# Stick-breaking attention dealt out between the rounds of a chunked recurrence, with the residual X kept in device memory meanwhile

## The reference

```python
h = h + 0.5 * swiglu(rms_norm(h, ffn1_norm), ...)             # feed-forward 1
proj = rms_norm(h, mix_norm) @ w_in
sb_out = stick_breaking_attention(q, k, v)                    # 8 heads of 64
rw_out = rwkv7_time_mix(proj[..., 3 * SB_WIDTH:], ...)        # 8 heads of 64
h = h + concatenate([sb_out, rw_out], -1) @ w_out
h = h + 0.5 * swiglu(rms_norm(h, ffn2_norm), ...)             # feed-forward 2

# stick-breaking attention, per block of queries
z = q_blk @ k.T * scale
log_keep = where(valid, -softplus(z), 0.0)
log_rest = cumsum(log_keep, reverse=True) - log_keep
attn = where(valid, exp(log_sigmoid(z) + log_rest), 0.0)
out = attn @ v

# rwkv7: a state S (64 x 64) per head, one step per token
sa = S @ -kk_t
S = S * w_t + outer(sa, kk_t * a_t) + outer(v_t, k_t)
y_t = S @ r_t
```

## Time and profile before

| what | us |
|---|---|
| median of 3 runs | 2483.41 (2479.57 to 2485.19) |
| profiled execution | 2484.07 |
| its span | 2482.1 |
| attention (559.27 to 614.27) | 55.00 |
| recurrence (614.27 to 738.67) | 124.40 |

### The profile page before, as it was taken

One profiled execution on the slowest core, in us unless ns is written; L12 is line 12 of the kernel. 1 busy time (PEld: TensorE's weight loads), 2 busy tenths in 40 slices (PEclk: granted clock), 3 DMA queues, 4 the chain that ended last, 5 costly groups with the idle time before them and its releaser, 6 DMA issues.

```text
span 2482.1 us, 48923 instructions
## 1 busy us (share of the span) xinstructions
PE 2433.5 (98%) x20393; PEld 2237.6 (90%) x20393; DVE 1706.8 (69%) x2927; ACT 1080.4 (44%) x1956; POOL 98.8 (4%) x108
## 2 busy tenths in 40 slices
PE   9999999999999999999999999999989999999998
PEld 7999999996887989898999999898877888989896
DVE  6877775646556879688879585243976445879694
ACT  5444343334434535356535243112874224535252
POOL 0000001000320000001000002000000000000001
PEclk9999999999999999999999999999999999999999
DMA  4233232220001332332232323222212323233322
GB/s 151 85 106 104 99 99 92 78 84 6 4 12 43 104 109 96 111 96 78 81 122 94 101 96 97 78 86 84 60 43 77 98 94 102 94 102 103 102 92 71
DMA packets 72378, 213.00 MB, mean 86 GB/s; under 512 B 12796, under 2 KB 20028, under 8 KB 72032
## 3 DMA queue, kind: packets, MB, share of 16 engines
q1 hardware_dynamic: 70496, 209.03, 26.0%
q0 software_dynamic: 480, 0.73, 0.1%
q10 hardware_dynamic: 1184, 0.12, 0.0%
HBM read 207.61 MB, written 2.20 MB: 85 GB/s over the span
## 4 chain that ended last, share of the span: by engine, by line
PE 87%; DVE 6%; ACT 4%; issue 2%; DMA 0%; DVEq 0%; ACTq 0%
PE PS L866 22%; PE PS L1401 20%; PE PS L1358 11%; PE PS L1360 11%; PE PS L1359 11%; DVE WL L951 1%; ACT WH L939 1%; PE PS L1236 1%; PE PS L2259 1%; PE PS L1709 1%; PE PS L1708 1%; PE PS L1710 1%; PE PS L2842 1%; DVE P L2905 1%; PE PS L2209 1%
## 5 line engine op out<-in xcount | busy, mean ns | idle before, releaser
L1358 PE MATMUL PS<-OPH,WH 128*128 128x256 f32 (+1 forms) x2112 | 604.5, 286 | 3.8 <-DVE OPL L1108 2.8
L1360 PE MATMUL PS<-OPH,WL 128*128 128x256 f32 (+1 forms) x2112 | 600.6, 284 | 0.0
L1359 PE MATMUL PS<-OPL,WH 128*128 128x256 f32 (+1 forms) x2112 | 598.9, 284 | 0.0
L939 ACT ACTIVATE WH<-WR 128x1024 fp32r<-128x1024 f32 (+2 forms) x277 | 275.5, 995 | 564.0 <-PE PS L866 272.6
L951 DVE TENSOR_TENSOR WL<-WR,WH 128x1024 fp32r<-128x1024 f32 (+2 forms) x277 | 318.7, 1151 | 190.1 <-ACT WH L939 190.0
L1358 PEld LDWEIGHTS PS<-OPH,WH 128*128 128x128 f32 x2112 | 402.1, 190 | 7.6 <-DVE OPL L1108 3.0
L1359 PEld LDWEIGHTS PS<-OPL,WH 128*128 128x128 f32 x2112 | 402.0, 190 | 1.9 <-issue 1.5
L1360 PEld LDWEIGHTS PS<-OPH,WL 128*128 128x128 f32 x2112 | 401.4, 190 | 0.0
L939 ACT ACTIVATE WH<-SUMS 128x512 fp32r<-128x512 f32 x352 | 210.9, 623 | 230.7 <-DVE SUMS L977 188.0
L951 DVE TENSOR_TENSOR WL<-SUMS,WH 128x512 fp32r<-128x512 f32 x352 | 234.7, 687 | 21.0 <-ACT WH L939 20.5
L866 PE MATMUL PS<-NHI,WH 128*128 128x264 f32 (+2 forms) x976 | 237.9, 309 | 1.5 <-ACT TMP L2633 1.0
(11 more groups left out here) (476 smaller groups left out, 4627.8 us busy)
## 6 DMA issues: line engine op xcount, KB each, us to landing
WR<-in_ffn_up SPq DMA_DIRECT2D x64, 512.0 KB, 4.0
WR<-in_ffn_down SPq DMA_DIRECT2D x64, 512.0 KB, 3.7
WR<-in_ffn_gate SPq DMA_DIRECT2D x56, 512.0 KB, 3.7
WR_MORE<-in_ffn_gate SPq DMA_DIRECT2D x32, 512.0 KB, 4.5
WR_MORE<-in_ffn_up SPq DMA_DIRECT2D x24, 512.0 KB, 4.1
WR<-in_ffn_down SPq DMA_DIRECT2D x32, 384.0 KB, 3.2
WR<-in_w_gate SPq DMA_DIRECT2D x24, 512.0 KB, 3.5
WR<-in_w_out SPq DMA_DIRECT2D x16, 512.0 KB, 3.6
```

Source lines behind the costliest of these rows:

```text
L939: e.activation(split_unit(i)[0][:, 0:w], src, ACT.Copy).then_inc(S["w_hi"], 1)
L1358: e.matmul(o, wh[:, at:at + 128], hi, start=k == 0 and s in (1, 2, 5), stop=False, skip_group_check=True)
L1359: e.matmul(o, wh[:, at:at + 128], lo, start=False, stop=False, skip_group_check=True)
L1360: last = e.matmul(o, wl[:, at:at + 128], hi, start=False, stop=k == 3, skip_group_check=True)
```

## The change

Attention is no longer a stage. Its sections are lists per round, and the three engines take them from there:

```diff
+        SB_SCANS = [(944, 1344), (0, 416), (416, 944)]
+        SB_DIFFS = [(416, 1343), (0, 416)]
+        BANKS_OF = {"z": 2, "t": 1, "v": 1}
+        ROUNDS, SB_ROUNDS = 4 * 8 + 16, 34
+        for p in range(4):
+            d = 1 + 7 * p
+            for half in range(2):
+                for y in range(4):
+                    breaking_at[d + 3 + 4 * half + y // 2].append(("t", p, half, y))
+            for part in range(2):
+                breaking_at[d + 9 + part].append(("v", p, part, 0))
+            for pos in range(3):
+                breaking_at[max(d - 2 + pos, 0)].append(("z", p, pos, 0))
+            for half in range(2):
+                for piece, late in (("scan", 0), 0), (("scan", 1), 0 + half), (("scan", 2), 1 + half), (("diff", 0), 2 + half), (("diff", 1), 2 + half):
+                    pieces_at[d + 3 * half + late].append((2 * p + half,) + piece)
```

A pair of heads takes seven rounds. The scan is cut in three pieces, the subtraction in two, the value product in two. On ScalarE and VectorE the sections and pieces of a round stand at the start of the next one; the copy into Y_S moves to ScalarE:

```diff
         def act_rwkv(e, q):
             for c, k in mixed_order:
+                if (c, k) in first_of_round:
+                    for item in breaking_at[4 * c + k - 1]:
+                        act_breaking(e, q, *item)
+                if c == 8 and k in (12, 13):
+                    q.wait_ge("outs", 7)
+                    q.wait_ge("sb_val", 4)
+                    act_split(e, q, U["w_out", k - 11])
...
         def dve_rwkv(e, q):
             for c, k in mixed_order:
+                if (c, k) in first_of_round:
+                    for item in pieces_at[4 * c + k - 1]:
+                        dve_breaking(e, q, *item)
+                if (c, k) == (8, 12):
+                    q.wait_ge("outs", 7)
+                    dve_split(e, q, U["w_out", 1])
```

```diff
+            def between_writers(last):
+                fences[0] += 1
+                last.then_inc(S["fence"], 1)
+                if waiting and taken[0] + BANKS_OF[waiting[0][0]] <= 3:
+                    taken[0] += BANKS_OF[waiting[0][0]]
+                    pe_breaking(e, q, *waiting.popleft())
+                q.wait_ge("fence", fences[0])
+
             for c, k in mixed_order:
+                if (c, k) in first_of_round:
+                    while waiting:
+                        pe_breaking(e, q, *waiting.popleft())
+                    waiting.extend(breaking_at[4 * c + k])
+                    taken[0] = 0
...
+                    if x < 4:
+                        for p, f, u in heads_in_turn:
+                            last = e.matmul(PS[f, bank, 64 * p:64 * p + 64], TU[u, 1, p], PM[u, p], start=p == 0,
+                                            stop=True, skip_group_check=True)
+                        between_writers(last)
                     for p, f, u in heads_in_turn:
-                        if x < 4:
-                            e.matmul(PS[f, bank, 64 * p:64 * p + 64], TU[u, 1, p], PM[u, p], start=p == 0,
-                                     stop=True, skip_group_check=True)
-                        last = e.matmul(PS[u, bank + 1, 64 * p:64 * p + 64], PM[u, p], TU[u, 1, p], start=p == 0,
-                                        stop=True, skip_group_check=True)
+                        last = e.matmul(PS[u, bank, 256 + 64 * p:320 + 64 * p], PM[u, p], TU[u, 1, p],
+                                        start=x == 4 and p == 0, stop=True, skip_group_check=True)
```

The first corners of step 1, which were already two runs of eight one after the other, have the same fence between them. The bonus products move to chunk 8:

```diff
+        RK_AT = {(8, 3 + 2 * i): i for i in range(4)}
+        BONUS_AT = {(8, 5 + 2 * i): i for i in range(4)}
```

For the space, X is stored to device memory during the projection and loaded again before the output projection; the values, the scan's result and a turned operand lie in its place. KEEPS (three heads) lies in the four weight slots WR, other tiles in WH and WL, so w_out 1 and 2 are fetched only when the last transposes are made:

```diff
+            for k in range(DT):
+                q.wait_ge("added", k + 1)
+                e.dma_start(x_kept[:, k, :], X[:, k, :]).then_inc(S["x_out"], 16)
+                sync_weights(e, q, shifted + k, shifted + k + 1)
+            sync_weights(e, q, shifted + DT, late)
+            q.wait_ge("x_out", 16 * DT)
+            q.wait_ge("sb_turn", 32)
+            sync_weights(e, q, late, late + 2)
+            q.wait_ge("sb_val", 4)
+            q.wait_ge("sb_diff", 16)
+            q.wait_ge("outs", 4)
+            for k in range(DT):
+                e.dma_start(X[:, k, :], x_kept[:, k, :]).then_inc(S["x_in"], 16)
```

More of the change, by code:

```diff
@@ L11 @@
+import collections
 import itertools
@@ new lines, in build @@
+        SMALL_0, at = place("SMALL0", at, 3, 4, CH)
+        chunk_homes.append(home + [SMALL_0[:, i] for i in range(3)])
+        home, _, at = of_home(1, at)
+        LT1, end = place("LT1", AFTER_TURNED, 4, CH)
+        assert end <= AT_WH + 2 * SLOT
+        VH1, end = place("VH1", AFTER_QK, 4, CH)
+        assert end <= AT_RKV - 4 * L
+        AT_HOME_2 = at
+        PM1, at = place("PM1", AT_HOME_2 + 2304, 4, CH)
+        STT, at = place("STT", at, 4, HD)
+        assert at <= FREE - 192
@@ L573, in build @@
+        RS, SA = (heads_of_rows(flat_tmp[:, 1536 + 256 * i:1792 + 256 * i]) for i in range(2))
+        ST, at = place("ST", AT_WA, 2, 4, HD)
+        assert at <= AT_WA + L
         Y_R, _ = place("Y_R", AT_RKV - 4 * L, 4, L)
-        assert at <= AT_RKV - 4 * L
         CEN, at = place("CEN", AFTER_BONUS, 4, L)
@@ L2248, in pe_rwkv @@
                     for p, f, u in heads_in_turn:
-                        last = e.matmul(PS[u, bank, 64 * p:64 * p + 64], XC[f, p, 0], BCV[f, 2, p], start=p == 0,
+                        last = e.matmul(PS[u, bank, 64 * p:64 * p + 64], XC[f, p, 0], BCV[2][f, p], start=p == 0,
                                         stop=True, skip_group_check=True)
@@ L2304, in pe_rwkv @@
                     for p, f, u in heads_in_turn:
-                        last = e.matmul(PS[f, bank, 64 * p:64 * p + 64], BCV[f, 0, p], SA[f, p], start=False,
+                        last = e.matmul(PS[f, bank, 64 * p:64 * p + 64], BCV[0][f, p], SA[f, p], start=False,
                                         stop=True, skip_group_check=True)
```

416 lines of the change are left out of this document (238 added, 178 removed).

## The result

The changed kernel takes 2522.62 us (median of 4 runs, 2519.14 to 2522.99); the kernel before, timed beside it, 2482.35 us (2479.57 to 2485.19). The ratio is 1.0163, 95% interval 1.015 to 1.0176: 40 us slower. The forecast was 2502 in a range of 2484 to 2518, so the direction was right and the size was not: +18 was forecast, +40 came.

A forecast was written before the change was run, and what follows sets the result against it. The prediction took TensorE, busy 98% of the span, as the bound, with almost no slack in full rounds. Its terms, -5.9 - 4 - 2 + 15.1 + 2.6 + 6.6 + 4 + 1.5, gave +17.9 on 2484.07: 2502 us, range 2484 to 2518.

The forecast's parts named there:

- Corners: 36 recurrence corners, split into two runs of eight products, need 0.94 us instead of 0.52: +15.1 us (13 to 17).
- Fences: TensorE's waits between a corner's two runs: 16 of 45 stay empty, at 0.2 us each; +2.6 us (1 to 8).
- Insertions: 52 attention sections enter between 64x64 products at 44 places, each shape change costing 0.15 us: +6.6 us (0 to 14).
- New waits: In-order TensorE waits at attention's transposes, scores or values for differences, banks or copies, some 0.5 us each: +4 us (1 to 12).
- slack of the filling rounds: Rounds before chunk 4 enters have 7.9 us of slack, which attention's work partly fills: -4 us (0 to -7).
- the tail: Four bonus products move from full rounds to rounds 37 to 43, where half finds slack: -2 us (0 to -4).
- the end: End of the recurrence: VectorE forms w_out 1's low part ahead of chunk 8's last corner: +1.5 us (0 to 3).
- X: Eight X stores between the projection's weight loads, and eight loads back after round 32, cost 0 (to +5) us.
- C: Rival, chance 0.16: in-order queues lock into each other at 15 round starts, the stage gets 18 us more: 2520 us.
- A: Rival, chance 0.06: TensorE has slack in the full rounds that hides corners' second half, shape changes and new waits: 2476 us.
- B: Rival, chance 0.14: fences, shape changes and waits overlap with each other, a filled fence having drained anyhow: 2486 to 2488 us.
- D: Rival, chance 0.04: X loads or weights behind them come late at the output projection, 5 to 10 us over forecast: 2510 us.

The follow-up runs named there:

- b1: Kernel before, with the sixteen products of each of 36 corners written as two runs of eight, no semaphore between: 2485.77 us, ratio 1.0007.
- b2: As b1, plus an empty semaphore wait between the two runs of the 36 corners and of the nine first corners: 2503.01 us, ratio 1.0072.
- e3: Changed kernel with no attention section inside a fence; all are issued at the next round's start and all 45 fences are empty: 2508.73 us, ratio 1.0099.
- e1: Changed kernel with all 52 attention sections issued ahead of round 0, as a stage of their own: 2529.52 us, ratio 1.0185.
- h1: Kernel before, with only the four bonus products and their VectorE steps moved to chunk 8's levels: 2483.5 us, ratio 1.0002.
- f1: Changed kernel with attention's transposes and values issued one round later, sections still going into fences: 2515.43 us, ratio 1.0141.
- b3: Kernel before, with single results taken in turn through three PSUM banks instead of four: 2486.56 us, ratio 1.0009.
- e2: As e1, with attention's three banks given to the single results from round 0 on, six in all: 2520.76 us, ratio 1.0151.
- g2: e3 with the two corners of a round woven, so another run of eight stands before a fence is waited for: 2507.24 us, ratio 1.0089.

## Why the prediction was wrong

By its own steps:

- *Corners, +15.1 (13 to 17).* The sum came near, the step failed. "The two runs need 2 x 0.47 = 0.94 instead of 0.52" took the start to start of two groups on the same quarters for that of any two groups. Runs on other quarters overlap by themselves: b1 cost 2 us. The profile before showed it, and I read past it. The earlier trace rows hold a half (645.30) of which only x10 of sixteen matmul rows stand in one line; the lines that follow it in the timeline have the rest, in turn with the next group (L2221):

```profile
645.54 0.27 PE L2221 MATMUL PS<-CHANNELS 64*64 64x64 f32 x2
645.59 0.28 PE L2259 MATMUL PS<-TU,TMP 64*64 64x64 f32 x3
645.65 0.22 PE L2221 MATMUL PS<-CHANNELS 64*64 64x64 f32 x1
```

- *Fences, +2.6 (1 to 8).* Priced at 0.2 us, and for the 16 empty ones only. A fence costs 0.39 us over two overlapping runs (b2), a filled one nearly as much (e3: 0.07 less), so all 45 count. Together with the corners the prediction had 17.7 us and the ledger has 18.3: two errors that cancelled, so the near sum is luck.
- *Insertions, +6.6 (0 to 14).* 0.15 a place; e3 against e1 gives 0.08, with the clock taken out. In the changed kernel the other groups take 88.7 us for e1's 86.7, with the same three banks, and attention's own products 2.1 more than before: some 4 us over 44 places, 0.09 each. Within the range, and below its middle. The Trainium skill's rule (TensorEngine Tiling (Array Packing), "Key Properties", a change of tiling mode drains the engine), read as two full drains of 0.16 us, would make 0.32 a place. No run here bears that out: it is four times what they show.
- *New waits, +4 (1 to 12), attention's idle time -5.9, slack of the filling rounds -4 and of the tail -2, the end +1.5.* Together -6.4; the ledger has idle time +10.5. This is the step that failed: 16.9 us, where the whole error in the stretch is 35.8 - 17.9 = 17.9. Only the last term was right; h1 shows nothing of the tail's -2. The prediction did name such waits, three transposes behind their differences and four places with a bank or a copy, at 0.5 us each, +4; there were 14 places at 1.0 on average, 13.8 us. "Their copies do not stand behind a section not yet issued" is true and beside the point: the sections stood ahead of the copies and differences that they need, ten of the 14 in fences, where TensorE could do nothing else. The prediction had named the bound, wrong upward if single waits on ScalarE or VectorE between rounds 8 and 32 sum to more than 8 us. They are 11.1 us, 9.2 of them for attention (the waits between 599.57 and 734.78, chunk 2's scores to chunk 8's):

```profile
PE PS L2119 <- DVE KEEPS L2174: 3.7, 5, 1.0
PE PS L2135 <- ACT AFTER L2156: 1.6, 1, 1.6
PE PS L2119 <- ACT Y_S L2160: 1.4, 2, 0.8
PE PS L2104 <- ACT AFTER L2156: 1.4, 2, 1.0
PE PS L2104 <- ACT KEEPS L2148: 1.1, 1, 1.1
PE PS L2350 <- DVE XC L2480: 1.0, 5, 0.2
PE PS L2350 <- DVE STT L2520: 0.9, 1, 0.9
```

  e3 and f1 show the waits for attention to be the cause: the idle time ahead of it fell from 13.8 to 2.7 and 7.1 us, and the kernel became 14 and 7 us faster, of which 7.0 and 4.0 stand in the profiled stretch. The full rounds were not where it missed most: from chunk 4's scores (646.32) to chunk 8's (733.68) they take 21.8 us a chunk, and 21 were forecast; 9.2 of the 13.8 us of waiting come before.
- *The filling rounds* gave nothing back: TensorE is busy 46.73 us of 55.80 there, four of the waits for attention, 6.2 us, stand in that window, and the idle time ahead of the recurrence's own groups is 8.4 us in the stretch where 7.5 stood. And the stage's own waits were replaced, not removed: even in e3, 10.2 us of idle time stand where 11.7 stood.
- *Three banks, not priced.* 2 to 4 us (b3, e2), which the smaller cost of the insertions about makes up. The prediction doesn't mention that the chunks' single results have one bank less.
- *The end, +1.5.* Right. The split (L982) stands ahead of chunk 8's last sum (L2502), which answers to the earlier trace rows:

```profile
769.83 1.22 DVE L982 TENSOR_TENSOR WL<-WR,WH 128x1024 fp32r<-128x1024 f32 x1
770.96 0.41 DVE L2502 TENSOR_TENSOR TU<-TU,PS 128x256 f32<-128x256 f32 x1
```

  In the earlier trace rows the sum began 0.78 us after ScalarE's last copy had ended. Here that copy (L2454, from 768.17) ends at 768.55, so it is 1.63 us later than it would have been.
- *X, 0.* No engine's wait in the profile after names its loads: right.
- *Rivals.* C (2520) was nearest in time and in kind, queues that lock into each other, though at 14 places, ten of them in fences, and not at 15 round starts; it had 0.16. A was half right: there was room that the busy share didn't show, in idle quarters rather than in time, and b1 went into it as A says. But what hid the split couldn't hide a fence, and A fell with b2. B (2486 to 2488) fell with the result; that a filled fence hides its cost is true of 0.07 us of 0.39 (e3). D did not occur.

## What to carry to other kernels

Before a group is priced, look at whether its row is whole in the timeline. Where rows of neighbours are split and interleaved, their products overlap in the array, and what an edit can lose is the overlap, which a wait took away here (17 us) and another order of writing hardly did (2 us). Work dealt into another stage's gaps on an engine in order should come well after its data, a round later here, not just ahead of the wait: the same sections one round later were 7 us better, and in no fence 14. Ask whether slack can be filled at all: idle time was 11.7 us before, and no kernel with attention dealt out came under 10.2. And before two traces are set against each other for a few us, compare how long TensorE had its lower clock in each: in e3 that was more than half of what an insertion seemed to cost.

## What the runs showed of the hardware

- Two runs of eight 64x64 products on opposite pairs of the array's quarters, written one after the other without a wait, start 0.31 us apart in b1 and cost at most 0.09 us a corner over sixteen written in turn (full rounds of b1; the ratio, 1.0007, is not clear of 1).
- TensorE waiting for its own last product costs 0.39 us against such a pair (b2, 45 places); with a run of eight others in between it is less, 0.10 to 0.14 by one pair of profiles (g2 against e3), which the times don't confirm.
- A wait for a PSUM bank that VectorE reads costs 0.2 us a place, six places in the changed kernel, and three banks for single results cost 2 to 4 us in all (0.84 us a chunk in full rounds against four banks in b3, 0.72 against six in e2).
- TensorE at a granted clock of 0.50 for 3.4 us makes a stage of unchanged work 1.5 us longer (attention in before and b3).
- Putting a section of other shapes between the groups of 64x64 products costs 0.08 to 0.09 us a place (e3 and the changed kernel against e1).
